# Layer 1's output projection: half of its inputs taken by pairs of row blocks with seven products, the gate folded into the last pass's weights

## The chip, the cores and the metric

The kernel runs on one core of one Trainium2 chip. The metric is the time of one execution on the device in microseconds (us), the median of several runs.

## The reference, cut to what matters

```python
# layer 1 (odd): x is (1024 tokens, 1024), POOL_WIDTH = 2048
proj = h @ w_in;  v, g = split(proj, 2)
mixed = einsum('bsgc,gcd->bsgd', window_mean(v) - v, w_grp) + b_grp
y = mixed * scale * silu(g)              # (1024, 2048)
x = x + gate * (y @ w_out)               # w_out is (2048, 1024), gate is one row of 1024
out = rmsnorm(x, final_g)
```

The change lies in the last two lines alone: the product of y (1024 tokens by 2048 inputs) with w_out (2048 by 1024), the gate, the residual and the final norm. Everything is float32. The kernel splits each operand into an upper part ("hi", rounded to the fp32r type) and what is left ("lo"), and makes three products hi\*hi, hi\*lo, lo\*hi in PSUM, so each block of 128 inputs, 128 rows and 512 columns is three matmuls.

## The kernel before

The work is written out by hand: each engine has its own ordered list of instructions, and they meet through semaphores. SyncE (SP) issues all the DMAs from one ordered list, so a DMA that waits holds back all that come later in the list. The engines' parts are these. ScalarE (ACT) makes the hi parts (`split_hi`, L880; `split_y`, L947) and copies some products out of PSUM. VectorE (DVE) makes the lo parts (`split_lo`, L1411; `split_y`, L1478), the sums that read PSUM, the residual and the final row. GpSimd (POOL) only makes the sums of the weights for the pairs described next (L841 to L852).

**Pairs.** Most projections ahead of this stage are done by pairs of output blocks with seven products in place of eight (`pair`, `product`, `last_of`). A pair q takes two blocks of weights, R1 and R2, through a ring of four raw buffers. POOL makes four sums of them, ACT and DVE split six operands, and TensorE (PE) makes the products in the order 1, 2, 5, 6, 3, 7, with product 4 of a pair put behind product 1 of the next. The other operand stays in the buffer X: for each kp four blocks and three sums of them (T1 to T3, and T4), also hi and lo. One product is 4 kp by 3 = 12 matmuls, one pair 84. The five copies or sums out of PSUM are `take_1`, `take_5`, `take_2`, `take_21` on ACT and `add_11`, `add_12`, `take_22` on DVE.

**The last mix.** In the stage ahead of the output projection PE makes M0 of the last group (`mix`, 24 matmuls), then product 4 of the last pair, then M1, M2 and M3. DVE closes each with `mixed(n, m)` (L2046), which reads PSUM and writes y, and SP spills y to the DRAM tensor `y_dram`.

**The output projection of layer 1.** It has two passes. Pass A makes the rows 0 to 3 (blocks of 128 tokens), pass B the rows 4 to 7. Each has 16 steps, one for each block of 128 inputs. In a step, y is the stationary operand, four row blocks by two halves of the columns by three matmuls = 24 matmuls, and the eight results stay in the eight banks of PSUM. Each step needs a block of w_out (512 KB, unit `("W", 1, p, k)`, raw ring of four) and half a row of y (256 KB). ACT and DVE split both (`step_splits`). The split operands have room for three steps, so the hi part of step n waits until PE has finished step n - 3. The last two steps of pass A and the last three of pass B are made block by block (`last_steps`), so that the blocks end one after the other. A step of pass A may write a bank only when the `mixed` that reads it is done (`free_bank`): block 1, half 1 and block 2, half 0 wait for M2's, block 3 for M3's.

**After a pass.** `residual(1, b)` makes, for each half, a product PSUM \* gate (L1864) and a sum with the old row (L1868). ACT squares the row and takes the root (L1184, L1187), DVE the reciprocal, and `row_out` (L1879) makes the final row. SP's `store(b)` writes it out. In pass B, rows 0 to 3 are finished behind the steps 3 to 7, and SP's stores stand between the loads of later steps.

Of the kernel before, what the change touches and what calls it, by code (L numbers as in the profile page):

```python
# [40 lines left out]
for _name, _n in ROWS_A + ROWS_B:  # L41
# [14 lines left out]
PAIRS += [(name, n) for n in range(GROUPS) for name in ("V01", "G01", "V23", "G23") if n or name[1] == "2"]  # L56
Q = {pair: q for q, pair in enumerate(PAIRS)}

# [6 lines left out]
        if PAIRS[q] != ("C", HEADS - 1) and not (PAIRS[q][0] == "V01")}  # L65
TIME_ORDER = [k + half * KB for k in range(KB) for half in range(2)]
GROUP_ORDER = [GB * g + m for g in GORDER for m in range(GB)]
# [3 lines left out]
           1: {b: (2 * (b % 4), 2 * (b % 4) + 1) for b in range(SB)}}  # L71
# [39 lines left out]
def build(nc, x, c, norm_g, mod_w, mod_b, hy_w_in, hy_conv_w, hy_conv_b, lru_w_a, lru_b_a, lru_w_x, lru_b_x,  # L111
# [41 lines left out]
    def last_steps(layer, p):  # L153


        blocks, steps = BLOCKS[layer, p], list(range(2 * KB - LAST[layer, p], 2 * KB))
# [30 lines left out]
    for q in range(3 * (HEADS - 1)):  # L187
        add_pair(q)
    STEPS = [(layer, p, k) for layer, p in BLOCKS
             for k in ((TIME_ORDER if layer == 0 else GROUP_ORDER) if p == "A" else range(2 * KB))]  # L190
    mods1 = [("m1", chunk, kk) for kk in range(KB) for chunk in range(2)]
    for layer in range(2):
        if layer == 1:
# [3 lines left out]
            for q in range(Q["V23", 0], len(PAIRS)):  # L197
                add_pair(q)
                if PAIRS[q][0] == "V01" or q == len(PAIRS) - 1:
# [4 lines left out]
        for n, (_, p, k) in enumerate(s for s in STEPS if s[0] == layer):  # L204
            LOADS.append(("W", layer, p, k))
# [26 lines left out]
    with ExitStack() as ctx:  # L232
# [67 lines left out]

        def flat(ap):
# [55 lines left out]
        def piece(at, width, dt=F32):  # L357
            if dt is F32R:
# [4 lines left out]
        Y_RAW = ([halves(bufs[:, 3 + n // 2, :])[:, n % 2, :] for n in range(YR)],  # L363
                 [piece(2 * KB * S + n * HALF, HALF) for n in range(YR)])
        at_y = 2 * KB * S + YR * HALF
        Y_HI = ([y_half(n, 0) for n in range(YS)], [piece(at_y + n * HALF, HALF, F32R) for n in range(YS)])
        Y_LO = ([y_half(n, 1) for n in range(YS)], [piece(at_y + (YS + n) * HALF, HALF, F32R) for n in range(YS)])
        at_rows = at_y + 2 * YS * HALF
        gate1, final = piece(at_rows, D), piece(at_rows + D, D)
# [3 lines left out]
        XR = ([bufs[:, (1, 6, 7, 9)[b % 4], :] for b in range(SB)], [piece(b * S, S) for b in range(SB)])  # L373
        XN = ([flat(whole_x[b % 4][:, 6, :, :]) for b in range(SB)], [piece((KB + b) * S, S) for b in range(SB)])

# [107 lines left out]
        half_done = sem("half_done")  # L483

# [2094 lines left out]
```

## Time and profile before

| | before |
|---|---|
| median of 3 runs | 1303.34 us (1303.34 to 1305.5) |
| the profiled execution | 1303.69 us, its span 1301.9 us |
| PE busy | 1278.3 us, 98% of the span |
| DVE busy | 937.8 us, 72% |
| ACT busy | 629.3 us, 48% |
| POOL busy | 272.9 us, 21%, nothing after 1079.0 us |
| mean granted TensorE clock | 0.992 |

The span runs from the first to the last instruction in the profiler's record. Times below are counted from its start. Busy time of PE counts overlapping matmuls once. An instruction's duration contains the time for which it waited for its operands' ports, but not the time for which it waited for a semaphore.

### The profile page before, as it was taken

Reading aid. Unit: us, or ns where it says so; the run is one execution under the profiler, and the core shown is the slowest. Engines: PE = TensorE matmul, PEld = TensorE weight load, DVE = VectorE, ACT = ScalarE, POOL = GpSimd, SP = SyncE. Lnnn points to the kernel's source line nnn. Section 1 sums busy time; section 2 is a strip of 40 time slices with the busy share of each in tenths; the row PEclk is TensorE's granted clock in tenths of the full one; section 3 lists DMA queues with packets and bytes.
Section 4 is the critical chain, followed back from the end, with each engine's and each line's share of the span. In section 5 each row is a group of like instructions: output and inputs, shape, how many; then the busy total and the mean of one; then the engine's idle time right before and its main releaser. Section 6 shows DMA issues by size and latency. Waiting matters only on the chain.

```text
span 1301.9 us, 15429 instructions
## 1 busy us (share of the span) xinstructions
PE 1278.3 (98%) x5687; PEld 1054.5 (81%) x5687; DVE 937.8 (72%) x1119; ACT 629.3 (48%) x888; POOL 272.9 (21%) x158
## 2 busy tenths in 40 slices
PE   5999999999999999999999999999999999999997
PEld 5877888888888888887888888888888888888886
DVE  6889987878878887777477698758758656434636
ACT  7466656464646465545567474144144143222522
POOL 0033443443534332000000023133133131000000
PEclk8999999999999999999999999999999999999999
DMA  9812233323232341697747202321321321864541
GB/s 289 219 49 69 83 116 98 105 65 113 69 114 75 108 134 46 227 380 263 269 162 271 81 18 77 101 81 33 113 82 34 112 81 38 309 243 146 176 155 65
DMA packets 145618, 171.51 MB, mean 132 GB/s; under 512 B 6598, under 2 KB 117382, under 8 KB 145544
## 3 DMA queue, kind: packets, MB, share of 16 engines
q1 hardware_dynamic: 145544, 170.53, 40.6%
q8 instruction: 46, 0.75, 0.2%
q14 instruction: 28, 0.23, 0.1%
HBM read 145.33 MB, written 25.17 MB: 131 GB/s over the span
## 4 chain that ended last, share of the span: by engine, by line
PE 89%; DVE 7%; issue 1%; SPq 1%; ACT 1%; DMA 0%; DVEq 0%; ACTq 0%
PE psum L2194 29%; PE psum L2196 29%; PE psum L2195 29%; DVE whole_x L1864 1%; DVE w_lo L1411 1%; DVE X L1501 1%; SPq L587 1%; PE psum L2329 1%; PE psum L2386 0%; SPq L576 0%; DMA whole_x<-in_mod_w 0%; ACT w_hi L880 0%; DVE bufs L1646 0%; DVE w_lo L1433 0%; DVE late L1494 0%
## 5 line engine op out<-in xcount | busy, mean ns | idle before, releaser
L2194 PE MATMUL psum<-X,w_hi 128*128 128x512 f32 x1140 | 446.4, 392 | 1.2 <-DVE X L1545 0.8
L2195 PE MATMUL psum<-X,w_hi 128*128 128x512 f32 x1140 | 444.6, 390 | 0.0
L2196 PE MATMUL psum<-X,w_lo 128*128 128x512 f32 x1140 | 444.5, 390 | 0.0
L2194 PEld LDWEIGHTS psum<-X,w_hi 128*128 128x128 f32 x1140 | 214.7, 188 | 48.2 <-issue 1.7
L2196 PEld LDWEIGHTS psum<-X,w_lo 128*128 128x128 f32 x1140 | 214.5, 188 | 44.7
L2195 PEld LDWEIGHTS psum<-X,w_hi 128*128 128x128 f32 x1140 | 214.6, 188 | 44.4 <-issue 0.2
L1411 DVE TENSOR_TENSOR w_lo<-raw,w_hi 128x1024 fp32r<-128x1024 f32 x98 | 120.6, 1230 | 157.4 <-ACT w_hi L880 156.9
L880 ACT ACTIVATE w_hi<-raw 128x1024 fp32r<-128x1024 f32 x98 | 103.6, 1057 | 199.7 <-PE psum L2196 160.7
L902 ACT ACTIVATE w_hi<-ssum 128x512 fp32r<-128x512 f32 x140 | 87.2, 626 | 120.2 <-PE psum L2196 86.2
L1433 DVE TENSOR_TENSOR w_lo<-ssum,w_hi 128x512 fp32r<-128x512 f32 x140 | 120.1, 865 | 22.0 <-ACT w_hi L902 21.4
L841 POOL TENSOR_TENSOR ssum<-raw 128x512 f32<-128x512 f32 x35 | 62.7, 1791 | 287.4 <-DMA raw<-in_pool_w_in 253.6
L849 POOL TENSOR_TENSOR ssum<-ssum,raw 128x512 f32<-128x512 f32 x35 | 55.8, 1593 | 309.9 <-DVE w_lo L1433 309.9
L2194 PE MATMUL psum<-w_hi,X 128*128 128x512 f32 x256 | 99.7, 389 | 0.3 <-DVE whole_x L1868 0.3
L2196 PE MATMUL psum<-w_hi,X 128*128 128x512 f32 x256 | 99.6, 389 | 0.0
L2195 PE MATMUL psum<-w_lo,X 128*128 128x512 f32 x256 | 99.6, 389 | 0.0
L852 POOL TENSOR_TENSOR ssum<-raw 128x512 f32<-128x512 f32 x35 | 78.5, 2242 | 78.7 <-DVE w_lo L1433 78.7
L846 POOL TENSOR_TENSOR ssum<-ssum,raw 128x512 f32<-128x512 f32 x35 | 62.1, 1774 | 47.2 <-DVE w_lo L1433 45.2
L1425 DVE TENSOR_TENSOR w_lo<-raw,w_hi 128x1024 fp32r<-128x1024 f32 x35 | 42.7, 1221 | 24.1 <-ACT w_hi L891 23.8
L2194 PEld LDWEIGHTS psum<-w_hi,X 128*128 128x128 f32 x256 | 48.0, 188 | 10.6 <-DVE whole_x L1868 0.7
L2196 PEld LDWEIGHTS psum<-w_hi,X 128*128 128x128 f32 x256 | 48.1, 188 | 10.0
L2195 PEld LDWEIGHTS psum<-w_lo,X 128*128 128x128 f32 x256 | 48.0, 188 | 10.0
L2194 PE MATMUL psum<-d_hi,w_hi 128*128 128x512 f32 x128 | 49.9, 390 | 0.3 <-DVE w_lo L1411 0.3
(244 smaller groups left out, 1953.3 us busy)
## 6 DMA issues: line engine op xcount, KB each, us to landing
raw<-in_hy_w_in SPq DMA_DIRECT2D x48, 512.0 KB, 5.1
raw<-in_hy_w_out SPq DMA_DIRECT2D x48, 512.0 KB, 5.0
raw<-in_pool_w_in SPq DMA_DIRECT2D x32, 512.0 KB, 5.0
raw<-in_pool_w_out SPq DMA_DIRECT2D x32, 512.0 KB, 4.2
aux<-in_mod_w SPq DMA_DIRECT2D x16, 512.0 KB, 4.1
y_dram<-bufs SPq DMA_DIRECT2D x16, 512.0 KB, 2.7
raw<-in_mod_w SPq DMA_DIRECT2D x16, 512.0 KB, 6.0
y_dram<-gb_ SPq DMA_DIRECT2D x16, 512.0 KB, 3.3
```

The costliest lines, as they stand in the source:

```text
L841: nc.gpsimd.tensor_tensor(even, a21, a22, ALU.add).then_inc(s_ready, 1)
L846: nc.gpsimd.tensor_tensor(odd, even, a11, ALU.add).then_inc(s_ready, 1)
L849: nc.gpsimd.tensor_tensor(even, odd, a12, ALU.add).then_inc(s_ready, 1)
L852: nc.gpsimd.tensor_tensor(odd, a21, a11, ALU.add).then_inc(s_ready, 1)
L880: nc.scalar.activation(flat(w_hi[:, es:es + 2, :]), raw[:, at, :], ACT.Copy).then_inc(hi_done, 1)
L902: nc.scalar.activation(w_hi[:, es, :], ssum[:, op % 2, :], ACT.Copy).then_inc(hi_done, 1)
L1411: nc.vector.tensor_tensor(flat(w_lo[:, es:es + 2, :]), raw[:, at, :], flat(w_hi[:, es:es + 2, :]).bitcast(F32), ALU.subtract).then_inc(lo_ ...
L1425: ins = nc.vector.tensor_tensor(w_lo[:, es:es + 2, :].rearrange("p two (k n) -> p two k n", k=KP), raw_blocks(q, 0), w_hi[:, es:es + 2, :] ...
L1433: ins = nc.vector.tensor_tensor(w_lo[:, es, :], ssum[:, op % 2, :], w_hi[:, es, :].bitcast(F32), ALU.subtract)
L2194: nc.tensor.matmul(out_, whi, xhi, start=first, stop=False, skip_group_check=check)
L2195: nc.tensor.matmul(out_, whi, xlo, start=False, stop=False, skip_group_check=check)
L2196: return nc.tensor.matmul(out_, wlo, xhi, start=False, stop=last, skip_group_check=check)
```

## The change

The 2048 inputs of the projection are split: the 8 blocks of groups 0 and 3 stay with the two passes, which now have 8 steps each, and the 8 blocks of groups 1 and 2 (`PAIRED`) are done by pairs of row blocks between the two passes, as 4 more pairs ("O", 0) to ("O", 3), with index OUT = 35 to 38. Here w_out is the operand that stays in X and y is what goes through the ring.

```diff
+PAIRS += [("O", j) for j in range(SB // 2)]
+OUT, LAST_GROUP = Q["O", 0], Q["G23", GROUPS - 1]
-GROUP_ORDER = [GB * g + m for g in GORDER for m in range(GB)]
+GROUP_ORDER = [GB * g + m for g in GORDER[:2] for m in range(GB)]
+PAIRED = range(GB, GB + KB)
+N_STEPS = (2 * KB, KB)
 # PE
+                if (layer, p) == (1, "B"):
+                    for q in range(OUT, len(PAIRS)):
+                        pair(q, after_1=(lambda: last_of(q - 1)) if q > OUT else None)
...
+                            if (layer, p, n, b, half) == (1, "B", 0, 5, 1):
+                                last_of(len(PAIRS) - 1)
```

SP loads the 8 blocks of w_out into X's raw places (2 for each kp), as soon as product 4 of the last group's pair has ended:

```diff
+            def out_weights(kp):
+                sp.wait_ge(full_of["4"], OUT)
+                for n in range(2):
+                    k = PAIRED[2 * kp + n]
+                    sp.dma_start(whole_x[kp][:, 2 * n:2 * n + 2, 1, :], ...).then_inc(out_in[kp], 16)
```

POOL makes T1 and T3 of each kp (8 subtractions of 128x512), DVE T2 and T4 (8 of 128x512), ACT the hi parts (`upper_out`, 2048 and 1536 columns for each kp) and DVE the lo parts (`low_out`, the same). On DVE they stand between the closings of the last mix and the splits:

```diff
             mixed(n, 0)
             step_splits(first[0])
             mixed(n, 1)
+            t2_and_t4_out(0)
             step_splits(first[1])
             mixed(n, 2)
+            t2_and_t4_out(1)
+            low_out(0)
             mixed(n, 3)
...
+            for n, step in enumerate(s for s in STEPS if s[0] == 1 and s[1] == "A"):
+                if n >= 2:
+                    step_splits(step)
+                if n in (2, 3):
+                    t2_and_t4_out(n)
+                if n in (2, 4, 5):
+                    low_out((n + 1) // 2 if n < 5 else 3)
```

The rows of a pair are finished by `add_rows` on DVE (two operations of 128x1024 for each row, all in SBUF), one pair later:

```diff
+            def add_rows(q, which):
+                ...
+                nc.vector.tensor_tensor(part, part, gate1, ALU.mult).then_inc(pair_part, 1)
+                ...
+                nc.vector.tensor_tensor(XR[1][b], XR[1][b], part, ALU.add).then_inc(pair_added, 1)
...
+                if q == len(PAIRS) - 1:
+                    step_splits(last[0])
+                add_12(q)
+                prep(q, 6)
+            take_22(len(PAIRS) - 1)
+            step_splits(last[1])
+            for n, step in enumerate(last):
+                if n < 2:
+                    add_rows(len(PAIRS) - 1, n)
+                else:
+                    step_splits(step)
+                if n in (3, 4, 5, 6):
+                    row_out(n - 3)
```

In pass B the gate goes into the weights. POOL multiplies each raw block of 128x1024 by the gate before ACT splits it, and `residual` of the rows 4 to 7 is a single sum of PSUM and row:

```diff
+            pool.wait_ge(gate_in, 32)
+            for k in GROUP_ORDER:
+                pool.wait_ge(raw_in[at], raw_landed(unit))
+                nc.gpsimd.tensor_tensor(raw[:, at, :], raw[:, at, :], gate1, ALU.mult).then_inc(gated_w, 1)
 # residual
+                    if (layer, b // 4) != (1, 1):
+                        ... part * gate
-                    nc.vector.tensor_tensor(XR[layer][b][:, cols], XR[layer][b][:, cols], XN[layer][b][:, cols],
+                    nc.vector.tensor_tensor(XR[layer][b][:, cols], XR[layer][b][:, cols], part, ALU.add)
```

SP's list for pass B. The first load of y waits until the third pair's rows are added (`pair_added` 6), since they lie in the same memory, and from step 4 on a store follows each load:

```diff
+            for n, step in enumerate(s for s in STEPS if s[0] == 1 and s[1] == "B"):
+                ring_load(("W",) + step)
+                y_load(step)
+                if n >= 4:
+                    store(n - 4)
```

Other buffers move too (y_lo lies over y_raw, so a load of y waits for PE's step four before it), and blocks 4 to 7 use other banks.

## Rows read from the trace of the kernel before

**Rows 1.** The page: span, busy time, chain that ended last by engine.
```profile
span 1301.9 us, 15429 instructions
PE 1278.3 (98%) x5687; PEld 1054.5 (81%) x5687; DVE 937.8 (72%) x1119; ACT 629.3 (48%) x888; POOL 272.9 (21%) x158
...
PE 89%; DVE 7%; issue 1%; SPq 1%; ACT 1%; DMA 0%; DVEq 0%; ACTq 0%
```

**Rows 2.** Stretches of pass A and pass B, PE busy, clock, DMA.
```profile
1119.24:1206.28 87.04, 87.04 (x386) 1.00 0.64 229
1206.28:1293.35 87.07, 86.81 (x383) 1.00 0.37 130
```

**Rows 3.** Timeline of PE: start, us; product 4's successor, first of pass A, last.
```profile
1102.92 0.39 PE L2194 MATMUL psum<-d_hi,w_hi 128*128 128x512 f32 x1
...
1119.24 0.39 PE L2194 MATMUL psum<-w_hi,X 128*128 128x512 f32 x1
...
1293.66 0.39 PE L2196 MATMUL psum<-w_hi,X 128*128 128x512 f32 x1
```

**Rows 4.** Timeline of the end: the last half row on DVE.
```profile
1294.68 0.68 DVE L1864 TENSOR_TENSOR whole_x<-psum,whole_x 128x512 f32<-128x512 f32 x1
1295.39 0.69 DVE L1868 TENSOR_TENSOR whole_x<-whole_x 128x512 f32<-128x512 f32 x1
```

**Rows 5.** Timeline of POOL and DVE, 1059 to 1080 us.
```profile
1059.25 1.28 POOL L841 TENSOR_TENSOR ssum<-raw 128x512 f32<-128x512 f32 x1
...
1073.94 2.22 POOL L849 TENSOR_TENSOR ssum<-ssum,raw 128x512 f32<-128x512 f32 x1 [6.51 <-DVE w_lo L1433]
...
1075.35 0.69 DVE L1462 TENSOR_TENSOR vp<-vp,psum 128x512 f32<-128x512 f32 x1 [0.34 <-DVE win L2015]
...
1076.64 1.23 DVE L2015 TENSOR_TENSOR win<-win 128x1038 f32<-128x1038 f32 x1
1076.79 2.22 POOL L852 TENSOR_TENSOR ssum<-raw 128x512 f32<-128x512 f32 x1 [0.63 <-DVE w_lo L1433]
1077.90 1.67 DVE L1433 TENSOR_TENSOR w_lo<-ssum,w_hi 128x512 fp32r<-128x512 f32 x1
```

**Rows 6.** Groups of DVE, 700 to 800 us: shapes, count, busy us, mean ns.
```profile
L1411 DVE TENSOR_TENSOR w_lo<-raw,w_hi 128x1024 fp32r<-128x1024 f32 x8 | 9.8, 1224 | 9.3 <-ACT w_hi L880 9.3
...
L1494 DVE SCALAR_TENSOR_TENSOR d_sums<-d_sums,whole_x 128x512 f32<-128x512 f32 x4 | 2.8, 692 | 0.1
```

**Rows 7.** Timeline of one step of pass B: hi and lo parts, final row.
```profile
1217.98 1.06 ACT L880 ACTIVATE w_hi<-raw 128x1024 fp32r<-128x1024 f32 x1 [2.49 <-PE psum L2196]
1218.95 0.62 ACT L947 ACTIVATE X<-whole_x 128x512 fp32r<-128x512 f32 x1
...
1219.08 1.23 DVE L1411 TENSOR_TENSOR w_lo<-raw,w_hi 128x1024 fp32r<-128x1024 f32 x1 [3.61 <-ACT w_hi L880]
1220.22 0.69 DVE L1478 TENSOR_TENSOR X<-whole_x,X 128x512 fp32r<-128x512 f32 x1
...
1221.01 1.28 DVE L1879 SCALAR_TENSOR_TENSOR whole_x<-whole_x,rstd 128x1024 f32<-128x1024 f32 x1
```

**Rows 8.** SP's timeline when product 4 of the last pair has ended, and two stores.
```profile
1103.17 0.34 SPq L664 DMA_DIRECT2D whole_x<-y_dram  x1
...
1222.33 0.34 SPq L696 DMA_DIRECT2D out<-whole_x  x1
1222.71 0.43 SPq L600 DMA_DIRECT2D raw<-in_pool_w_out  x1
```

**Rows 9.** The page's DMA issues: count, KB each, median us from issue to landing.
```profile
raw<-in_pool_w_out SPq DMA_DIRECT2D x32, 512.0 KB, 4.2
...
raw<-in_mod_w SPq DMA_DIRECT2D x16, 512.0 KB, 6.0
```

**Rows 10.** A stretch with full DMA queues: clock, DMA share, GB/s.
```profile
1230.00:1236.00 6.00, 1.00 1.01 374
```

**Rows 11.** Timeline of DVE ahead of pass A.
```profile
1109.73 1.23 DVE L1411 TENSOR_TENSOR w_lo<-raw,w_hi 128x1024 fp32r<-128x1024 f32 x1 [2.41 <-ACT w_hi L880]
1110.87 0.68 DVE L1478 TENSOR_TENSOR X<-whole_x,X 128x512 fp32r<-128x512 f32 x1
1111.47 1.28 DVE L2046 SCALAR_TENSOR_TENSOR gb_<-psum,vec,gb_ 128x1024 f32<-128x1024 f32 x1
...
1119.44 1.28 DVE L2046 SCALAR_TENSOR_TENSOR gb_<-psum,vec,gb_ 128x1024 f32<-128x1024 f32 x1 [3.76 <-PE psum L2196]
```

**Rows 12.** The last 9 us: busy us of each engine, then the clock.
```profile
1293.00:1302.00 9.00, 1.04 (x5) 0.54 (x3) 5.86 (x10) 2.55 (x9) 0.00 (x0) 0.80 0.44 175
```

More of the change, by code:

```diff
@@ L153, in last_steps @@
     def last_steps(layer, p):
-        blocks, steps = BLOCKS[layer, p], list(range(2 * KB - LAST[layer, p], 2 * KB))
+        blocks, steps = BLOCKS[layer, p], list(range(N_STEPS[layer] - LAST[layer, p], N_STEPS[layer]))
         order = [(n, b, half) for b in blocks for half in range(2) for n in steps]
@@ L483, in build @@
         half_done = sem("half_done")
+        out_in = [sem(f"out_in{kp}") for kp in range(KP)]
+        out_hi = sem("out_hi")
+        out_lo = sem("out_lo")
+        pair_part = sem("pair_part")
+        gated_w = sem("gated_w")
+        pair_added = sem("pair_added")
         def v(name, n=0, count=1):
@@ L605, in ring_load @@
                     which = "R1 R2".split().index(kind)
-                    if name in PAIR_L0:
+                    if name == "O":
+                        rows = slice((2 * n + which) * P, (2 * n + which + 1) * P)
+                        load(y_dram[1, PAIRED[0]:PAIRED[-1] + 1, :, rows].rearrange("k p n -> p k n"), KB)
+                    elif name in PAIR_L0:
                         load(columns(hy_in, L0_COLS[PAIR_L0[name][which]] * D + n * P), KB)
@@ L1378, in _, with upper_out @@
             step_splits(first[1])
-            passes(1, 2)
+            def upper_out(kp):
+                act.wait_ge(t24_added, 2 * (2 * KP + kp) + 2)
+                act.wait_ge(t13_added, 2 * (2 * KP + kp) + 2)
+                for blocks in (slice(0, 4), slice(4, 7)):
+                    nc.scalar.activation(X[:, kp, blocks, 0, :], whole_x[kp][:, blocks, 1, :], ACT.Copy).then_inc(out_hi, 1)
+            for n, step in enumerate(s for s in STEPS if s[0] == 1 and s[1] == "A"):
+                if n >= 2:
+                    step_splits(step)
+                if n in (1, 2, 3, 4):
+                    upper_out(n - 1)
+            load_root()
+            first_operands(OUT)
+            last = [s for s in STEPS if s[0] == 1 and s[1] == "B"]
+            for q in range(OUT, len(PAIRS)):
+                prep(q, 0)
+                take_1(q)
+                if q > OUT:
+                    take_21(q - 1)
+                prep(q, 1)
+                prep(q, 2)
+                take_5(q)
+                prep(q, 3)
+                take_2(q)
+                prep(q, 4)
+                prep(q, 5)
+                if q == len(PAIRS) - 1:
+                    step_splits(last[0])
+                prep(q, 6)
+            step_splits(last[1])
+            take_21(len(PAIRS) - 1)
+            for n, step in enumerate(last):
+                if n >= 2:
+                    step_splits(step)
+                if n in (2, 3, 4, 5):
+                    squares(1, n - 2)
             for b in range(4, SB - 1):
@@ L2299, in part_of @@
                 name = ("O", layer, b, half)
-                ins = products(area(name), Y_HI[layer][at % YS][:, rows], Y_LO[layer][at % YS][:, rows],
-                               w_hi[:, es + half, :], w_lo[:, es + half, :], n == 0, n == 2 * KB - 1)
-                if n == 2 * KB - 1 and name in FULL:
+                end = n == N_STEPS[layer] - 1
+                ins = products(area(name), y_hi(y_step)[:, rows], y_lo(y_step)[:, rows], w_hi[:, es + half, :],
+                               w_lo[:, es + half, :], n == 0, end)
+                if end and name in FULL:
                     ins.then_inc(psum_full, 1)
@@ L2552, in _ @@
                     part_of(y_steps[n], b, half)
-                for n in range(ends, 2 * KB):
+                for n in range(ends, N_STEPS[layer]):
                     behind(layer, p, n)
```

225 lines of the change are left out of this document (168 added, 57 removed).

## The prediction

> **What bounds the kernel now.** I read the page first. TensorE (PE) is busy for 98% of the span and has 89% of the chain that ended last; VectorE (DVE) has 72%, GpSimd (POOL) 21% [rows 1]. Then the stretches of the output projection: PE is busy for 87.04 of 87.04 us in pass A and 86.81 of 87.07 in pass B, at a granted clock of 1.00 [rows 2]. So any matmul that is left out is time gained, and any time for which PE waits is time lost, one for one. The timeline gives the pitch: the last mix has 72 matmuls in 16.32 us, the projection 767 steps from matmul to matmul in 174.42 us, so 0.227 us for one [rows 3]. A block product (3 matmuls) is 0.68 us, a step of 24 is 5.44, a product of a pair (12) 2.72, a pair of seven 19.0.
>
> **What is removed: matmuls.** Half of the projection was 8 blocks of inputs x 8 rows x 2 halves x 3 = 384 matmuls. Four pairs of 84 are 336. 48 x 0.227 = **-10.9 us**. All 48 lie on PE's path, so this is sure if PE stays fed.
>
> **What is removed: the end.** The last half row took a product (1294.68) and a sum (1295.39, to 1296.08) on DVE, and the product began 0.63 after the last matmul's end at 1294.05, since the product and sum of the half before were still at work [rows 3, 4]. With one sum per half, at 0.69 each, DVE is free when the last half comes: its sum ends near 1294.05 + 0.04 + 0.69 = 1294.8. What follows it stays. **-1.3 us**. Together -12.2 us.
>
> **What is added, and its cover.** Copies out of PSUM, hi and lo parts of the four pairs are the load that PE carries without a gap in the pairs before. In a pair of 19.0 us DVE has one lo part of 1024 columns and five of 512 (about 4.7), three sums (2.1) and four operations of `add_rows` at 1.22 (4.9), together 11.7; POOL has four sums at 1.28 [rows 5, 6]. I cost the pairs' own stretch at nothing. If that cover is gone, a pair loses at most the 5.1 us of POOL's sums. ACT's extra hi parts in pass A (3.6 us for a kp, four times, at 1.06 for 1024) find room, since a step of 5.44 us takes 1.7 of it [rows 7]. If it had none, the splits behind them would come late by 3.6 us, which is about the lead that they have.
>
> Two places are left, and both hang on one thing that the trace shows: **POOL and DVE wait for each other.** A POOL sum of 512 columns takes 1.28 us alone. At 1076.79 it began while DVE had an operation with two inputs in SBUF (1076.64, 1.23 us), and took 2.22. DVE's next, which alone takes 0.69, was then started at 1077.90 and took 1.67, to 1079.57: POOL's end at 1079.01 plus its own time. But the sum that DVE made of SBUF and PSUM at 1075.35 took its usual 0.69, with POOL at work until 1076.16 [rows 5]. So operations with two SBUF inputs on DVE and POOL's sums take turns, each whole. The Trainium skill ("SBUF — State Buffer", Who interferes with whom) says that a VectorE instruction with two SBUF inputs and a GpSimd instruction that reads SBUF exclude each other for the whole instruction, whoever is first. By that rule these places cost what follows; without it 1.5 us in all. The rows agree with it.
>
> *Place 1, ahead of pass A.* SP may issue the loads of w_out at 1103.2, when product 4 has ended [rows 8]. A 512 KB load lands 4.2 us after its issue [rows 9], and full queues move 374 GB/s [rows 10], 1.05 MB in 2.8 us: kp 0 lands near 1108, kp 1 at 1110.7, kp 2 (behind a step's 0.79 MB) near 1115.5, kp 3 at 1118.4. So POOL's eight subtractions (8 x 1.28 = 10.2 us at least) fall into 1108 to 1124. DVE begins its list at 1109.73 [rows 11]: split of step 0 (1.74), closing of M1 (1.2, PSUM, free of turns), two subtractions (1.4), split of step 1 (1.74), closing of M2 (1.2), two subtractions (1.4), lo parts of kp 0 (2048 and 1536 columns, 4.0), closing of M3 (1.3). Sum 14.0, so without turns M3's is done at 1123.7. PE wants block 3's banks at 1119.24 + 6 x 0.68 = 1123.3: 0.4 us late. With turns, six of POOL's eight go between DVE's operations and the rest behind the PSUM ones: 0.9 + about 5.4 more, so 1130.0, **6.2 to 6.7 late** (the first part of it, 1.9, already at M2's banks). Queued behind: all splits of pass A, but they keep 3 us of slack. I take 6.2; bounds 0.4 and 8.
>
> *Place 2, the last pass.* New is one POOL product of 1024 columns for each of 8 steps. The trace has none; from two sums of 512 it is at most 2.56, and at least 1.28; I take 2.45. The Trainium skill ("GPSIMD Engine Reference", Elementwise — side-by-side cycle accounting) gives 4497 ns for a two-input operation of 2048, so by estimate 2.25 for 1024; place 2 would be 1 to 2 us cheaper. I count from the pass's first matmul. The third pair's rows are added near -6.3 (product 2 of the last pair ends at -10.9, then a sum, two operations of 1.2 and a turn of POOL), and only then does SP issue y of step 0 and the loads behind it. The blocks 1 to 4, with their y, land at -2, 0, 2 and 4 by the rate above. DVE has, in its order: split 1, the four operations of `add_rows`, split 2, split 3, row 0, split 4, row 1: about 14.7 us, with POOL's gates 2 to 4 (7.4 us) taking turns from 0.8 on. So split 1 is ready at 7.5 (wanted at 8.2, product 4 lies inside step 0), `add_rows` ends at 14.7, split 2 at 16.4 where step 2 is wanted at 13.6: **2.8 late**. Row 0 is done at 19.5, row 1 at 22.6. SP's store(0) stands ahead of the load of block 5, store(1) of block 6, store(2) of block 7. So block 5 is issued at 20.0, lands at 24.4, is gated at 26.9; block 6 lands at 27.5 and its gate takes its turn ahead of block 5's lo part, which ends at 31.2; row 2 ends at 33.2; block 7 is issued at 33.6, lands at 38.0, is gated at 40.6 and split at 43.5 (hi, lo and y's lo 2.9 [rows 7]). Step 7 is wanted at 34.0 + 2.8 = 36.8: **6.7 late**. Together 9.5; with a load of 3.8 in place of 4.4 behind a store it is 8.3. I take 9.0. Without turns the same walk gives 0 to 1.2. With landings of 6.0 [rows 9] it gives about 13.
>
> **The sum** against the profiled span: 1301.9 - 10.9 - 1.3 + 6.2 + 9.0 = 1304.9, +3.0. On the median of the runs, which is 0.35 below the profiled execution, 1303.34 + 3.0 = **1306.3 us**. What decides the sign is whether PE's waits come to more than 12.2.
>
> **Rivals.**
> (b) *One place only, or half of each.* POOL's turns fall while DVE waits for ACT or PE anyhow; in the last pass the gates run well ahead of the splits and the walk's step from store to load is shorter. For it: most of the walk's waits are sums of small leads. PE then waits 5 to 12 us: 1296 to 1303. Against it: DVE's lists have no gap in either place.
> (c) *Faster, all hidden.* One mechanism: DVE is not held by POOL, the lo parts come as in the splits of today, 1.1 us after ACT's start. PE waits about 1.5: 1292.6. It decides below 12.2 us of waits, so it wins clearly if an exclusion costs DVE less than half an operation of POOL. Against it stands the 1.67.
> (d) *Slower still.* Either each pair also loses POOL's turns at its start (up to 5 us over four pairs), or the clock falls in one of the waits. It stayed at 1.00 through both passes, and was 0.80 on the mean of the last 9 us, with PE busy for 1.04 [rows 2, 12]. At its lower level each matmul would take twice 0.227, so 10 us at it cost 5: 1309.5 to 1315.
>
> **Chances and range.** Forecast (1303 to 1309.5) 0.5; (b) 0.25; (c) 0.1; (d) 0.15. The range leaves out (c) and a third of (d): 1296 to 1312. A measurement of this kernel tells about 0.2% from no change, 2.6 us: faster is below 1300.7, slower above 1305.9. Faster: (c) and 0.15 of (b), 0.25. Same: 0.10 of (b) and 0.18 of the forecast, 0.28. Slower: 0.47.
>
> **What the profile after would show.** PE's matmuls 48 fewer, at the same pitch. Two waits of PE on DVE's closings of M2 and M3 early in pass A, 6 us together, and POOL's subtractions there at 1.3 to 2.3 us each, with DVE's lo parts above 1.23. In the last pass a wait ahead of step 2 and one ahead of step 7, the load of its block issued right behind the store of row 2, and POOL's products at 2.4 us or more. After the last matmul about 6.8 us to the end in place of 7.85. If the pairs' own stretch has waits of PE, the cover that I counted at nothing was missing. I am wrong if PE's waits are under 10 or over 17 us, the likeliest cause being a gate's real length and the landing of loads behind stores.

## The result, and the profile after

| | before | after |
|---|---|---|
| median | 1303.34 us | 1312.2 us (1308.59 to 1314.47, 5 runs) |
| the profiled execution, its span | 1303.69, 1301.9 us | 1312.86, 1311.1 us |
| ratio of the times | | 1.0062, 95% interval 1.005 to 1.0073 |

The change made the kernel slower by 0.6%: 1.0062 x 1303.34 = 1311.4 us. The forecast was 1306.3 with a range to 1312.0, so the sign was right and the size fell short by 5 us. The result lies at the very end of the range: the median of the runs, 1312.2, is 0.2 above it. The changed kernel's runs differ by 5.9 us among themselves, and what follows is read from one of them.

The page after, beside [rows 1]: 48 matmuls fewer, PE's busy share lower and DVE's chain share higher, and the clock line, 9 throughout the projection before, shows an 8 at two places.

```profile
span 1311.1 us, 15456 instructions
PE 1274.1 (97%) x5639; PEld 1049.4 (80%) x5639; DVE 992.3 (76%) x1147; ACT 642.3 (49%) x904; POOL 333.3 (25%) x190
...
PEclk8999999999999999999899999999999999899998
...
PE 82%; DVE 9%; DMA 3%; issue 2%; SPq 1%; ACT 1%; POOL 0%; POOLq 0%; DVEq 0%; ACTq 0%
```

The waits of PE (waited for: us in total, times, longest). These are the projection's: three waits for VectorE, where PE was idle for 0.26 us in all before [rows 2].

```profile
PE psum L2396 <- DVE y_lo L1610: 8.0, 2, 5.0
PE psum L2396 <- DVE gb_ L2171: 4.9, 1, 4.9
```

The timeline of PE (start, us). From start to start the three gaps are 5.32, 3.42 and 5.38, less the pitch of 0.227 each: 5.1, 3.2 and 5.15. The matmul behind a wait takes 0.8 and the next ones 0.63, and they start 0.43 apart in place of 0.227. The last matmul, at 1304.14, leaves 6.96 us to the span's end, where before it was 8.24 [rows 1, 3].

```profile
1125.22 0.39 PE L2398 MATMUL psum<-w_hi,y_lo 128*128 128x512 f32 x1
1130.54 0.80 PE L2396 MATMUL psum<-w_hi,y_hi 128*128 128x512 f32 x1 [4.93 <-DVE gb_ L2171]
1131.13 0.63 PE L2397 MATMUL psum<-w_lo,y_hi 128*128 128x512 f32 x1
1131.56 0.63 PE L2398 MATMUL psum<-w_hi,y_lo 128*128 128x512 f32 x1
...
1263.36 0.76 PE L2396 MATMUL psum<-w_hi,y_hi 128*128 128x512 f32 x1 [3.02 <-DVE y_lo L1610]
...
1290.46 0.77 PE L2396 MATMUL psum<-w_hi,y_hi 128*128 128x512 f32 x1 [4.99 <-DVE y_lo L1610]
...
1304.14 0.39 PE L2398 MATMUL psum<-w_hi,y_lo 128*128 128x512 f32 x1
```

Stretches behind each wait and one that ends in a wait (columns as in [rows 2], with each engine's busy us and, third from the end, the clock): the granted clock falls once matmuls run again.

```profile
1131.00:1140.00 9.00, 9.00 (x29) 7.07 (x29) 8.93 (x10) 4.76 (x4) 0.00 (x0) 0.68 0.88 313
1260.00:1270.00 10.00, 6.97 (x25) 5.39 (x24) 9.37 (x12) 2.91 (x5) 0.00 (x0) 0.83 0.27 91
1280.00:1290.00 10.00, 5.47 (x25) 4.19 (x23) 5.00 (x7) 1.64 (x3) 2.34 (x1) 1.00 0.51 184
1290.00:1300.00 10.00, 9.54 (x35) 7.79 (x36) 5.08 (x8) 2.89 (x6) 0.00 (x0) 0.83 0.07 27
```

**One number for each kernel.** From the first matmul of the last mix to the last matmul, before took 1293.66 - 1094.63 = 199.03 us. Without 48 matmuls it would be 188.1. What a kernel takes above 188.1 is what it lost, in waits and in matmuls that come late behind them. (In the stretch before, one start came 0.66 behind the last one, at 1211.49, so 0.4 of waiting is in the 188.1; a kernel with no wait at all would show a loss of -0.4.) After took 1304.14 - 1096.46 = 207.7, so it lost **19.5**: 13.4 in the three waits and the other 6.1 nearly all in slow matmuls behind them. The balance against before is -10.9 + 19.5 - 1.3 (the end) + 1.8 = +9.1, beside a span longer by 9.2. The 1.8 is the start of the last mix, 1096.46 for 1094.63. It is no part of the change: in the profiled executions of kernels with the same instructions up to there it lay anywhere from 1092.4 to 1096.5.

**Place 1.** These are timelines of POOL and DVE where M3's closing (L2171) came late. DVE's operations with two operands in SBUF took 1.66 to 1.78 for the 0.69 of [rows 5, 6], POOL's subtractions 1.7 to 2.3 for 1.28.

```profile
1110.41 1.30 POOL L948 TENSOR_TENSOR whole_x<-whole_x 128x512 f32<-128x512 f32 x1 [29.57 <-DMA whole_x<-in_pool_w_out]
1111.67 2.27 POOL L950 TENSOR_TENSOR whole_x<-whole_x 128x512 f32<-128x512 f32 x1
...
1123.73 1.74 POOL L950 TENSOR_TENSOR whole_x<-whole_x 128x512 f32<-128x512 f32 x1
```

```profile
1111.57 1.22 DVE L1543 TENSOR_TENSOR w_lo<-raw,w_hi 128x1024 fp32r<-128x1024 f32 x1 [2.41 <-ACT w_hi L973]
1112.71 1.78 DVE L1610 TENSOR_TENSOR y_lo<-y_raw,y_hi 128x512 fp32r<-128x512 f32 x1
...
1122.65 1.67 DVE L2306 SCALAR_TENSOR_TENSOR whole_x<-whole_x 128x512 f32<-128x512 f32 x1
1124.24 5.04 DVE L2314 TENSOR_TENSOR X<-whole_x,X 128x2048 fp32r<-128x2048 f32 x2
1129.21 1.27 DVE L2171 SCALAR_TENSOR_TENSOR gb_<-psum,vec,gb_ 128x1024 f32<-128x1024 f32 x1
```

**Place 2.** In the last pass POOL's product (L960) takes 2.34 to 2.40 alone, and three of them together took 8.57. DVE's lo parts meanwhile took 3.06 and 2.89, and the first operation of `add_rows` 3.43. Later DVE stood idle twice, for 5.50 and 4.96, until a late block had been loaded, multiplied and rounded.

```profile
1245.08 2.39 POOL L960 TENSOR_TENSOR raw<-raw,d_sums 128x1024 f32<-128x1024 f32 x1 [11.08 <-DMA raw<-in_pool_w_out]
1248.16 8.57 POOL L960 TENSOR_TENSOR raw<-raw,d_sums 128x1024 f32<-128x1024 f32 x3 [0.69 <-DMA raw<-in_pool_w_out]
...
1285.03 2.34 POOL L960 TENSOR_TENSOR raw<-raw,d_sums 128x1024 f32<-128x1024 f32 x1 [6.57 <-DMA raw<-in_pool_w_out]
```

```profile
1248.60 3.06 DVE L1543 TENSOR_TENSOR w_lo<-raw,w_hi 128x1024 fp32r<-128x1024 f32 x1 [1.25 <-ACT w_hi L973]
1251.57 2.89 DVE L1610 TENSOR_TENSOR y_lo<-y_raw,y_hi 128x512 fp32r<-128x512 f32 x1
1254.39 3.43 DVE L2335 TENSOR_TENSOR d_sums<-d_sums 128x1024 f32<-128x1024 f32 x1
...
1262.53 0.68 DVE L1610 TENSOR_TENSOR y_lo<-y_raw,y_hi 128x512 fp32r<-128x512 f32 x1
...
1274.97 1.23 DVE L1543 TENSOR_TENSOR w_lo<-raw,w_hi 128x1024 fp32r<-128x1024 f32 x1 [5.50 <-ACT w_hi L973]
...
1279.11 1.28 DVE L2013 SCALAR_TENSOR_TENSOR whole_x<-gb_,rstd,d_sums 128x1024 f32<-128x1024 f32 x1
...
1288.49 1.22 DVE L1543 TENSOR_TENSOR w_lo<-raw,w_hi 128x1024 fp32r<-128x1024 f32 x1 [4.96 <-ACT w_hi L973]
```

Row 2 ends at 1280.4 on DVE, and SP issues its store at once and the load of block 7 behind it. The block is gated from 1285.03 on, 4.2 after its issue, and split from 1288.49: the chain of the walk.

```profile
1280.43 0.34 SPq L746 DMA_DIRECT2D out<-whole_x  x1
1280.81 0.43 SPq L640 DMA_DIRECT2D raw<-in_pool_w_out  x1
```

### The profile page after: what moved, and what is told of

It reads as the page before. It is cut to its first block, busy times and chain, and to the rows that moved or that the text cites. A ratio compares the mean times of both kernels' runs of the same rounds, so it can differ in the third digit from the quotient of the medians.

```text
span 1311.1 us, 15456 instructions
## 1 busy us (share of the span) xinstructions
PE 1274.1 (97%) x5639; PEld 1049.4 (80%) x5639; DVE 992.3 (76%) x1147; ACT 642.3 (49%) x904; POOL 333.3 (25%) x190
## 4 chain that ended last, share of the span: by engine, by line
PE 82%; DVE 9%; DMA 3%; issue 2%; SPq 1%; ACT 1%; POOL 0%; POOLq 0%; DVEq 0%; ACTq 0%
PE psum L2396 27%; PE psum L2397 26%; PE psum L2398 26%; DMA raw<-in_hy_w_out 2%; DVE w_lo L1543 2%; ACT w_hi L973 1%; DMA raw<-in_pool_w_out 1%; DVE y_lo L1610 1%; DVE X L1633 1%; SPq L627 1%; PE psum L2543 1%; PE psum L2600 0%; DMA whole_x<-in_mod_w 0%; SPq L616 0%; POOL raw L960 0%
## 5 line engine op out<-in xcount | busy, mean ns | idle before, releaser
L2396 PE MATMUL psum<-X,w_hi 128*128 128x512 f32 x1252 | 489.9, 391 | 1.2 <-DVE X L1677 0.8
L2397 PE MATMUL psum<-X,w_hi 128*128 128x512 f32 x1252 | 487.8, 390 | 0.0
L2398 PE MATMUL psum<-X,w_lo 128*128 128x512 f32 x1252 | 487.7, 390 | 0.0
L2396 PEld LDWEIGHTS psum<-X,w_hi 128*128 128x128 f32 x1252 | 235.4, 188 | 52.2 <-issue 1.6
L2398 PEld LDWEIGHTS psum<-X,w_lo 128*128 128x128 f32 x1252 | 235.4, 188 | 49.4
L2397 PEld LDWEIGHTS psum<-X,w_hi 128*128 128x128 f32 x1252 | 235.4, 188 | 48.5 <-issue 0.2
L2396 PE MATMUL psum<-w_hi,y_hi 128*128 128x512 f32 x128 | 53.0, 414 | 12.9 <-DVE y_lo L1610 8.0
L2397 PE MATMUL psum<-w_lo,y_hi 128*128 128x512 f32 x128 | 52.1, 407 | 0.0
L2398 PE MATMUL psum<-w_hi,y_lo 128*128 128x512 f32 x128 | 51.8, 404 | 0.0
L2163 DVE SCALAR_TENSOR_TENSOR gb_<-gb_,vec,win 128x1024 f32<-128x1024 f32 x16 | 20.5, 1284 | 38.9 <-ACT win L1373 38.9
L2397 PE MATMUL psum<-d_lo,w_hi 128*128 128x512 f32 x128 | 49.8, 389 | 0.0
L2398 PE MATMUL psum<-d_hi,w_lo 128*128 128x512 f32 x128 | 49.8, 389 | 0.0
```

Of the source, the lines that this page charges most:

```text
L2396: nc.tensor.matmul(out_, whi, xhi, start=first, stop=False, skip_group_check=check)
L2397: nc.tensor.matmul(out_, whi, xlo, start=False, stop=False, skip_group_check=check)
L2398: return nc.tensor.matmul(out_, wlo, xhi, start=False, stop=last, skip_group_check=check)
```

## The experiments

All are edits of the changed kernel. "Lost" is the time above 188.1 us as defined above; "waits" are PE's gaps of 0.4 us or more from the last mix on, in order, with what they stand ahead of. "M3" is the first matmul of pass A that writes block 3's banks, which waits for the closing of M3. "Mix" lies earlier: there the last mix's own matmuls for M3 wait for the closing of M1. Lost and waits are read from one execution of each kernel, while its runs differ by 2.4 to 7.5 us, so small differences in these two columns mean little.

| run | median us | ratio to before, 95% interval | lost | waits |
|---|---|---|---|---|
| the changed kernel | 1312.2 | 1.0062 (1.005 to 1.0073) | 19.5 | M3 5.1; step 2 3.2; step 7 5.15 |
| e1_m3_first | 1304.15 | 1.0001 (0.9992 to 1.0009) | 12.1 | step 3 of pass A 1.27; step 2 2.97; step 6 1.10; step 7 5.27 |
| e2_stores_last | 1306.11 | 1.0014 (1.0006 to 1.0023) | 15.5 | mix 1.2; M3 5.27; step 2 5.50 |
| e3_rows_late | 1308.62 | 1.0036 (1.0024 to 1.0048) | 17.6 | mix 0.5; M3 5.09; step 6 1.0; step 7 6.1 |
| e4_all_orders | 1302.04 | 0.9982 (0.9972 to 0.9991) | 9.1 | mix 0.9; end of pass A 2.2, 0.7; last pass 1.2, 2.7 |
| e5_pool_later | 1306.69 | 1.0021 (1.0012 to 1.0031) | 14.9 | M3 1.9; 0.4; step 2 3.2; step 7 3.4 |
| e6_no_gate | 1297.94 | 0.9962 (0.9949 to 0.9976) | 7.6 | M3 5.1 |
| e7_orders_and_sums | 1296.94 | 0.9948 (0.9936 to 0.9961) | 3.6 | end of pass A 1.15, 2.05 |
| e8_gate_in_sums | 1299.89 | 0.9975 (0.9964 to 0.9987) | 7.4 | M3 5.2 |
| e9_gate_in_sums_finer_order | 1293.17 | 0.9914 (0.99 to 0.9928) | 0.9 | mix 1.3 |
| e10_finer_order_gpsimd_gate | 1295.89 | 0.9936 (0.9924 to 0.9948) | 4.4 | mix 0.4; step 7 2.6 |
| e11_gate_on_vectore | 1298.31 | 0.9965 (0.9953 to 0.9977) | 7.6 | last pass 0.4, 2.7, 2.7 |
| e12_gate_on_vectore_ahead | 1292.51 | 0.9915 (0.9901 to 0.9928) | 0.7 | mix 1.1 |

**e1: M3's closing first.**

```diff
             mixed(n, 2)
+            mixed(n, 3)
             t2_and_t4_out(1)
             low_out(0)
-            mixed(n, 3)
```

> Only VectorE's list ahead of pass A is changed: the closing of M3 stands ahead of the two subtractions and the lo parts of kp 1 and kp 0. The changed kernel had TensorE wait 5.1 us there for M3's closing, and then run 14 matmuls at the lower clock (3.0 us). Theory 1 (the order of VectorE's list, with GpSimd's turns, sets the wait): M3's closing ends near 1123 in place of 1130.4, the wait and the slow matmuls go; since the list's total is the same, the splits of steps 2 and 3 end where they did, 1132 and 1139, and TensorE waits 0 to 2 us at step 3 in place of it: 5 to 8 us less than the changed kernel. Rival (the load of the weights, so GpSimd's subtractions, or the last mix itself are late): M3's closing moves by less than 2 us, no gain over 2 us.

The wait of 5.1 and its slow matmuls went, 7.4 us less lost. Part of the lateness moved: 1.27 at step 3 and 1.10 more in the last pass.

**e2: the stores of rows 0 to 3 behind the last load.**

```diff
                 y_load(step)
-                if n >= 4:
-                    store(n - 4)
-            for b in range(4, SB - 1):
+            for b in range(SB - 1):
                 store(b)
```

> Only SyncE's list in the last pass is changed: the stores of rows 0 to 3 stand behind the last load. Theory 1 (the loads of blocks 5 to 7 are late because each stands behind a store that waits for a row): block 7 is issued about 9 us earlier, the wait of 5.15 us ahead of step 7 and its 8 slow matmuls (1.8 us) go, the wait of 3.2 ahead of step 2 stays: 7 us less. Rival (GpSimd's product itself is what makes step 7 late): the block lands earlier, but the wait ahead of step 7 stays above 2 us, gain under 4.

Step 7's wait went, but step 2's grew from 3.2 to 5.5, and the gain was 6.1 us in place of the 7 expected. The loads that no store holds back brought a fourth product of POOL under `add_rows`, whose four operations took 3.42, 3.31, 1.21 and 3.26. The stores had kept POOL off DVE's way.

**e3: the last pair's rows added behind the splits 5 and 6.**

```diff
-                if n < 2:
-                    add_rows(len(PAIRS) - 1, n)
-                else:
+                if n >= 2:
                     step_splits(step)
+                if n in (5, 6):
+                    add_rows(len(PAIRS) - 1, n - 5)
```

> Only the last pair's add_rows is moved on VectorE, from ahead of the split of step 2 to behind the splits of steps 5 and 6 (nothing needs those rows before the residual of rows 6 and 7). Theory 1 (VectorE's list is full ahead of step 2): the wait of 3.2 us at step 2 and 7 slow matmuls (1.6 us) go; the rows and so the loads behind the stores come about as much earlier as the pass does, so the wait ahead of step 7 stays at 4 to 6 us: 4 to 5 us less. Rival (step 2 is late because block 2 lands or is gated late): the wait at step 2 stays above 1.5 us.

Step 2's wait went, and the waits ahead of the steps 6 and 7 grew from 5.15 to 7.1 in sum: DVE's work had only been moved ahead of the row whose store holds the last load. The gain was 3.6 us where 4 to 5 were expected.

**e4: e1 to e3 together, with DVE's sums and lo parts of w_out spread over later steps.**

```diff
-                if n in (2, 3):
-                    t2_and_t4_out(n)
-                if n in (2, 4, 5):
-                    low_out((n + 1) // 2 if n < 5 else 3)
+                if n in (2, 3, 4):
+                    t2_and_t4_out(n - 1)
+                if n in (2, 4, 5, 7):
+                    low_out((2, 4, 5, 7).index(n))
```

> All three orders together, with the lo parts of kp 0 to 3 spread one step later over pass A. GpSimd still makes its subtractions and the gate's products. Theory 1 (each of TensorE's waits is an order in a list): TensorE waits under 1 us in the whole projection, no slow matmul before the end; 12.2 us less than the kernel before, plus what the profile has in its early part by chance: 1291 to 1293. Rival (turns between VectorE and GpSimd cost time wherever they fall): 1296 or more, with new waits of TensorE behind splits that took over 1.9 us.

The expectation was missed by 9 us or more, and its rival came. Lateness came back at two ends: near the end of pass A, where POOL's sums for the pairs now met DVE's splits (lo parts of 2.31 and 1.75 for 1.22 and 0.69), and in the last pass, where y's lo part took about 2.89 five times beside a product of POOL. New orders alone had not removed the turns.

**e5: POOL's subtractions of the last two kp wait for M3's closing.**

```diff
             for kp in range(KP):
+                if kp == 2:
+                    pool.wait_ge(mixed_done, GB * GROUPS)
```

> From the changed kernel: GpSimd's subtractions for kp 2 and 3 wait until M3 is closed; nothing else is changed, VectorE's list is the same. Theory 1 (the two engines take turns, each operation whole): the three operations of VectorE ahead of M3's closing that took 1.0 to 1.1 us too long (y's lo part, T4 of kp 1, lo parts of kp 0) take their own time, M3's closing ends 3.2 us earlier, TensorE waits 1.9 us for it in place of 5.1 and has fewer slow matmuls: 3 to 5 us less. Rival (those operations are long for another reason, the DMAs' writes or ScalarE's reads of the same buffer): they stay long and the wait stays at 4.5 to 5.5 us.

DVE's list is the same as in the changed kernel, with POOL idle from 1114.3 to 1124.2. Three operations ahead of M3's closing, which POOL had made long, have their own length again, 0.68, 0.69 and 3.95 in place of 1.78, 1.67 and 5.04, and M3's wait is 1.9 in place of 5.1. The 1.9 that is left is about what POOL's first four subtractions, which still ran there, cost DVE earlier in the list: 1.79 and 1.67 for two operations of 0.69.

```profile
1115.86 0.68 DVE L1612 TENSOR_TENSOR y_lo<-y_raw,y_hi 128x512 fp32r<-128x512 f32 x1
...
1118.37 0.69 DVE L2308 SCALAR_TENSOR_TENSOR whole_x<-whole_x 128x512 f32<-128x512 f32 x1
1118.98 3.95 DVE L2316 TENSOR_TENSOR X<-whole_x,X 128x2048 fp32r<-128x2048 f32 x2
1122.85 1.28 DVE L2173 SCALAR_TENSOR_TENSOR gb_<-psum,vec,gb_ 128x1024 f32<-128x1024 f32 x1
```

**e6: no product on POOL.** The weights of the last pass stay as loaded, so the rows 4 to 7 lack the gate on half of their inputs.

> From the changed kernel: GpSimd's eight products are left out in the last pass, so rows 4 to 7 lack the gate on half of their inputs; all orders stay, the stores stand ahead of the loads. Theory 1 (the gate's turns and its delay between landing and split make both waits of the last pass): VectorE's list from the first split to row 1 is about 7 us shorter, the wait at step 2 is under 0.5 us, the one ahead of step 7 0 to 2 us, few slow matmuls: 9 to 11 us less than the changed kernel. Rival (the waits come from SyncE's list and VectorE's own work alone): one of the two waits stays above 2.5 us.

No wait is left in the last pass. The median is 14.3 us below the changed kernel's, where 9 to 11 were expected. All of place 2 hangs on these eight products; this run alone doesn't say whether by their turns with DVE or by their own time in the chain.

**e8: the gate back in the sums,** the first half of the change alone.

```diff
-                nc.gpsimd.tensor_tensor(raw[:, at, :], raw[:, at, :], gate1, ALU.mult).then_inc(gated_w, 1)
 # residual
-                    if (layer, b // 4) != (1, 1):
+                    if True:
```

> From the changed kernel: the gate goes back into the residual of rows 4 to 7 (a product and a sum for each half), GpSimd makes no product of the weights; the pairs stay. It is the first half of the change alone. Theory 1: as without the gate (both waits of the last pass nearly gone), and after the last matmul 1.3 us more: 8 to 10 us less than the changed kernel, so about as fast as the kernel before or up to 2 us slower, since place 1's 8 us stay. Rival (VectorE's extra products cost as much as the turns did): less than 5 us gained.

The first half is worth -0.25%, 3.3 us; the second half turned that into +0.62%, so it cost 11.4. The run was expected about as fast as the kernel before or up to 2 us slower, so it came out better than expected: no wait is left in the last pass, although DVE has the products of the sums to make again.

**e7: e4's orders with the gate in the sums.**

> The three orders of the earlier run together with the gate in the residual, no product on GpSimd. Theory 1: the waits of 1.2 and 2.7 us ahead of steps 6 and 7 that the three orders alone still had come from the gate's turns (y's lo parts of 2.89 us), and go; the one of 2.9 us at the end of pass A stays, since GpSimd's sums for the first pair of rows cause it; the end is 1.3 us longer: 3 to 5 us less than the three orders alone, 1297 to 1299. Rival (VectorE is full there by itself): a wait above 2 us stays ahead of step 6 or 7.

The last pass is free of waits and the end of pass A isn't, as expected: of its two waits the longer, 2.05, comes behind lo parts of 1.77 and 2.30 beside POOL's first sums for the pairs.

**e9: the gate in the sums, and pass A's work dealt out finer.** DVE's order is e4's in pass A with `low_out` in the steps 2, 3, 5, 7.

```diff
 # ACT
-                if n in (1, 2, 3, 4):
-                    upper_out(n - 1)
+                if n in (1, 2, 3, 5):
+                    upper_out((1, 2, 3, 5).index(n))
 # POOL, ahead of the sums for the new pairs
+            pool.wait_ge(ylo_done, Y[1, "A", GROUP_ORDER[-1]] + 1)
```

> The changed kernel with the gate back in the residual sums (the first half of the change alone) and with VectorE's, ScalarE's and GpSimd's orders in pass A's part of the projection dealt out: M3's mixed copy ahead of the leftover steps, the differences and sums of the lo parts one per step, ScalarE's high parts one per step, and GpSimd's sums for the outputs behind the last step of pass A. Theory (the time still lost after the 48 matmuls went is VectorE and ScalarE work standing ahead of what TensorE wants in pass A, and the matmuls at 0.43 us apart behind it): no wait over 0.5 us in the projection, no slow matmuls behind one; beside the first half alone (1299.89, where a wait of 5.17 us stood) some 8 us less: 1290 to 1293 us, ratio 0.990 to 0.992. Rival (VectorE is full in pass A, so an order only moves its lateness, as in the run with four orders changed): waits of 2 to 4 us in sum near the end of pass A, 1296 us or more, ratio 0.994 or more.

This came as expected but for one wait of 1.3. The windows show PE full through pass A at clock 1.00, with DVE busy for 37.52 of 40.19 us:

```profile
1119.81:1160.00 40.19, 40.19 (x179) 33.30 (x178) 37.52 (x32) 22.10 (x22) 9.64 (x5) 1.00 0.94 325
```

The one wait of PE from 1100 us on stands in the last mix, ahead of pass A. M3's matmuls wait for the closing of M1, and DVE's split ahead of that closing took 2.38 and 1.77 for its usual 1.22 and 0.69:

```profile
1110.53 2.38 DVE L1541 TENSOR_TENSOR w_lo<-raw,w_hi 128x1024 fp32r<-128x1024 f32 x1 [2.41 <-ACT w_hi L971]
1112.83 1.77 DVE L1608 TENSOR_TENSOR y_lo<-y_raw,y_hi 128x512 fp32r<-128x512 f32 x1
1114.52 1.27 DVE L2169 SCALAR_TENSOR_TENSOR gb_<-psum,vec,gb_ 128x1024 f32<-128x1024 f32 x1
```

```profile
1115.94 0.47 PE L2392 MATMUL psum<-d_hi,w_hi 128*128 128x512 f32 x1 [1.19 <-DVE gb_ L2169]
```

**e10: the same order in pass A, the product still on POOL, with the edits of e2 and e3.**

> The same finer order in pass A's part, with the gate's product left on GpSimd as in the changed kernel, the last pass's first four stores behind its last load, and its last pair's row sums behind the splits. It tests whether the second half of the change can pay at all once its lateness is reordered away. Theory (a 1024-wide product on GpSimd makes VectorE's small operations of the same time take 2.89 instead of 1.1 to 1.2 us, and that can't be ordered away while VectorE has no spare time): waits of 1.2 and 2.7 us in the last pass stay as in the run with four orders changed, with some slow matmuls behind them, against a tail 1.3 us shorter; 1295 to 1298 us, 3 to 5 us more than the kernel with the gate in the sums and the same order. Rival (the second half is worth its 1.3 us of tail once the orders are right): within 1 us of the kernel with the gate in the sums, or below it.

The ratio is 0.22% above e9's and the intervals just overlap; by the medians it is 2.7 us, where 3 to 5 were expected. There is one wait of 2.6 with eight slow matmuls. The theory's 1.2 us wait did not appear. Its DVE shows the turns again at the start of the last pass:

```profile
1238.64 2.87 DVE L1542 TENSOR_TENSOR w_lo<-raw,w_hi 128x1024 fp32r<-128x1024 f32 x1 [0.95 <-ACT w_hi L972]
1241.43 2.89 DVE L1609 TENSOR_TENSOR y_lo<-y_raw,y_hi 128x512 fp32r<-128x512 f32 x1
1244.24 3.43 DVE L1542 TENSOR_TENSOR w_lo<-raw,w_hi 128x1024 fp32r<-128x1024 f32 x1
```

**e11: the product on DVE, right ahead of the block's hi and lo part,** with e9's order.

```diff
+            def gate_block(step):
+                ...
+                nc.vector.tensor_tensor(raw[:, at, :], raw[:, at, :], gate1, ALU.mult).then_inc(gated_w, 1)
```

> The finer order, with the gate's product of each of the last pass's eight weight blocks made by VectorE ahead of that block's lo part (the rest of the second half of the change stays: one sum per half row at the end). The same work stands in the same chain from load to hi part; only GpSimd has none of it. Theory (what the second half costs in the last pass are the turns that VectorE and GpSimd take): VectorE's operations keep 0.69 and 1.22 us, the products take 1.22, no wait of TensorE over 0.5 us in the last pass, and the tail stays at 6.96: about 1.3 us below the kernel with the gate in the sums and the same order (ratio 0.9914), so 1290 to 1293 us, ratio 0.9895 to 0.991. Rival (the product in the chain from load to hi part costs it, on whatever engine, since the late blocks 5 to 7 come behind stores): waits of 2 to 3 us ahead of steps 5 to 7 as with GpSimd, ratio 0.993 or more.

The theory fell. There are no turns, every operation has its own length, and PE still waits 5.8 us. DVE makes the product (L1616), stands idle for 1.12 until ACT has the hi part, and only then makes the lo part (L1538). Between them stand the final rows (L2014), whose stores hold the loads of the blocks 5 to 7. DVE's list before row 0 had grown by the products and the idle times, and row 0 came 18.1 us after the pass's first matmul (1252.35 for 1234.29) where e9 had 11.7 (1250.19 for 1238.46). So the turns are one way in which the product makes DVE late, and not the only one.

```profile
1261.38 1.23 DVE L1538 TENSOR_TENSOR w_lo<-raw,w_hi 128x1024 fp32r<-128x1024 f32 x1 [1.13 <-ACT w_hi L968]
1262.52 0.68 DVE L1605 TENSOR_TENSOR y_lo<-y_raw,y_hi 128x512 fp32r<-128x512 f32 x1
...
1263.32 1.28 DVE L2014 SCALAR_TENSOR_TENSOR whole_x<-gb_,rstd,d_sums 128x1024 f32<-128x1024 f32 x1
1264.52 1.22 DVE L1616 TENSOR_TENSOR raw<-raw,d_sums 128x1024 f32<-128x1024 f32 x1
1266.86 1.23 DVE L1538 TENSOR_TENSOR w_lo<-raw,w_hi 128x1024 fp32r<-128x1024 f32 x1 [1.12 <-ACT w_hi L968]
```

**e12: the product on DVE one step ahead,** the stores behind the last load, the last pair's rows added behind the splits 2 and 3, the final rows behind the splits 4 to 7.

```diff
+            gate_block(last[1])
+            gate_block(last[2])
             step_splits(last[1])
             for n, step in enumerate(last):
+                if n >= 2:
+                    if n < len(last) - 1:
+                        gate_block(last[n + 1])
                     step_splits(step)
+                if n in (2, 3):
+                    add_rows(len(PAIRS) - 1, n - 2)
+                if n in (4, 5, 6, 7):
+                    row_out(n - 4)
```

> The gate's products on VectorE again, but each one step ahead of the lo part of its block, so that VectorE doesn't stand idle for ScalarE's hi part; the stores of the first seven rows behind the last load, so that no load hangs on a row; the last pair's rows added behind the splits 2 and 3, and the final rows 0 to 3 behind the splits 4 to 7. Theory (second form: what the gate's product costs is the chain from row to store to load to product to hi and lo part, and VectorE's full list ahead of it, on whatever engine the product is; the turns only lengthen it on GpSimd): with both gone no wait of TensorE over 0.5 us in the last pass and the tail at 6.96: ratio 0.9895 to 0.991, 1290 to 1293 us. Rival (VectorE has no room for eight more operations of 1.22 us at the turn from the last pair to the last pass): a wait of 1 us or more ahead of steps 1 to 3, ratio 0.993 or more.

No wait is left in the last pass, the last matmul stands 6.94 us from the end, and the median is the lowest of all. Its ratio of 0.9915 is no better than e9's 0.9914: the 1.3 us of the end are less than the intervals can tell.

## Why the prediction was right, and where it fell short

The time fell inside the stated range by less than its own uncertainty, and not by the forecast case. It lies in the 1309.5 to 1315 of rival (d). So the range held in part by luck; the terms one by one:

**Matmuls, -10.9.** Right: 48 fewer, at 0.227.

**The end, -1.3.** Right: from the start of the last matmul to the end 6.96 after 8.24, -1.28. Counted from its end, as the prediction did, it is 6.57 after 7.85; the 6.8 given among the signs was a slip.

**The pairs' own stretch, nothing.** Right: PE has no wait of 0.2 us or more there in any of these kernels, so DVE's and POOL's extra work for the four pairs is covered in that stretch. POOL's first sums for the pairs did cost something ahead of it where other work had moved there, at the end of pass A in e4 and e7.

**Place 1, 6.2.** Wait measured: 5.1. The list was counted at 20.3 us from its start to the end of M3's closing and took 18.9 (1111.57 to 1130.48). The 1.9 expected at M2's banks wasn't there, in this kernel or any other. The 0.9 to 1.3 of e2, e4, e9 and e12 stand earlier, ahead of the last mix's matmuls for M3: the prediction has M1's closing in DVE's list, but not who waits for it. Before, that closing ended at 1112.75, by the pitch 0.9 ahead of M3's first matmul; in the changed kernel it ended at 1115.69 and PE went on at 1115.84, 0.2 late. The Trainium skill's rule ("SBUF — State Buffer", Who interferes with whom), an exclusive lock between such VectorE and GpSimd instructions, agrees with both places, and e5 is its test at the first: with POOL moved away, the same operations took 0.68 in place of 1.78 and 3.95 in place of 5.04, and 3.2 of the 5.1 us of wait were gone.

**Place 2, 9.0.** Waits measured: 3.2 and 5.15, 8.35 together. Counted from the pass's first matmul at 1246.46, the walk had `add_rows` end at 14.7 (measured 15.0), split 2 at 16.4 (16.8), row 0 at 19.5 (19.9), row 2 at 33.2 (33.9), block 7 issued at 33.6 (34.4) and split at 43.5 (43.9). The product, taken at 2.45, is 2.34 to 2.40. Step 7's wait is under the 6.7 because PE came to it later than at 36.8: its own slow matmuls behind the first wait had used that time. The cause named for the loss was right too: without the products (e6, e8, e9) the last pass has no wait. How much of it was the turns and how much the product's own time between load and split is not shown: no run has one without the other. One argument against (b), that DVE's lists have no gap, was wrong here: DVE stood idle for 5.50 and 4.96 us behind late blocks.

**The term that was missing: slow matmuls behind a wait.** The forecast gave a wait its own length. Rival (d) had the clock falling in a wait, "10 us at it cost 5", at a chance of 0.15 together with another cause. All three waits brought it, some 6.1 us on 13.4. Waits of 13.4 against a gain of 12.2 would have been +1.2, and +3.0 with the 1.8 by which the profiled execution came late to the last mix; the slow matmuls are the step from there to +9.2. So the forecast case (1303 to 1309.5) was not what came: place by place its waits were right to within 1.1 us, and (d)'s clock came on top. The 1.8 is chance, and so is a part of how near the single terms came. The other half of (d), turns at the start of each pair, did not happen. The Trainium skill too ("TensorE: Matmul & The Clock Gate", HAM oscillation) has TensorE fall back to half its rate over idle gaps between matmuls; the trace agrees for these three waits, with 0.43 for 0.227, and not for every wait of the experiments.

**The rivals (b) and (c).** Waits under 12.2 in total need one of the places gone. e8 shows it: place 2 away, lost 7.4, 0.9975. (c), no exclusion, is excluded by e5.

**What the change is worth in parts.** The pairs alone gain 0.25% as written (e8) and 0.86% once the work in pass A is dealt out (e9): 1293.17 us, 0.9 of the 10.9 us lost. The gate in the weights gains 1.3 us at the end and costs more than that where its product makes something late. On balance it cost 11.4 us as changed, 0.22% in e10 against e9, and nothing that can be told in e12, whose product is on VectorE one step ahead and whose loads hang on no row. e9 and e12 are both faster than the kernel before and the changed one; which of the two is faster these runs can't tell. That e12's gain over e11 (0.9965 to 0.9915) comes from the product's place, the stores or the later rows was not taken apart, since it changed all three; nor was a product on POOL tried with e12's orders.

## What to carry to other kernels

Work that goes to an idle engine can still cost the full one, where their operations take turns as GpSimd's and VectorE's with two operands in SBUF did here: look at what the moved work takes turns with, and what is queued behind that. Where TensorE is full, price its waits above their length (here, from waits to loss, 10.6 to 12.1 us in e1, 13.4 to 19.5 in the changed kernel, 8.9 to 14.9 in e5). Ask also how little slack the moved work has in the order of its own engine: closing M3 first and dealing out the rest about one piece per step was worth 6.5 us of loss here (7.4 in e8, 0.9 in e9), with not an instruction less. A rearranged order is worth trying only on the one list that is late: e2 and e3 each removed the wait that they were aimed at and made another longer.

## What the runs showed of the hardware that wasn't expected

The granted clock fell behind short waits too, and not by their length alone. Behind the five waits of about 5 us ahead of M3's bank (the changed kernel, e2, e3, e6, e8) 9 to 13 matmuls came 0.43 us apart, and the clock of e8's stretch 1121 to 1131 was 0.68. Behind e1's of 5.27 in the last pass there were five, and behind e5's of 3.2 there twelve, so the number doesn't follow the length. Behind e10's wait of 2.6, ended at 1273.45, five matmuls came at the full pitch first, and only then eight at 0.43. But behind e1's wait of 2.97, e4's of 2.72, e7's of 2.05 and e11's first of 2.74 no matmul was slow, while e5's of 1.9 had slow ones behind it, from the fifth matmul on, and e11's second of 2.66, which ended 5.5 us behind the first, had seven. Waits of 1.3 us or less standing alone (e1, e7, e9, e12) had none. What decides between them stays open. In the changed kernel, the 10 us that ended in the longest wait were granted 1.00 with PE busy for 5.47 of them, and the 10 us behind them 0.83.
